# Cross attention of a fp32 transformer trunk: plain fp32 operands in scores and values in place of split halves of queries, keys, values and probabilities

## The reference

```python
def memory_cross_attention(h, mem_n, w_q, w_kv, w_o):
    B, S, _ = h.shape
    M = mem_n.shape[1]
    q = (h @ w_q).reshape(B, S, XA_HEADS, HEAD_DIM)
    kv = (mem_n @ w_kv).reshape(B, M, 2, XA_HEADS, HEAD_DIM)
    s = jnp.einsum('bshd,bmhd->bhsm', q, kv[:, :, 0]).astype(jnp.float32) * HEAD_DIM ** -0.5
    p = jax.nn.softmax(s, axis=-1)
    o = jnp.einsum('bhsm,bmhd->bshd', p.astype(kv.dtype), kv[:, :, 1])
    return o.reshape(B, S, XA_HEADS * HEAD_DIM) @ w_o
```

## Time and profile before

| what | value |
|---|---|
| median of 3 runs | 2618.49 us (2615.28 to 2619.13) |
| the profiled execution, its own time | 2622.67 us |
| its span, first to last instruction | 2620.9 us |
| mean granted TensorE clock in it, as a share of full speed | 0.966 |
| busy: TensorE, VectorE, ScalarE | 94%, 57%, 43% of the span |

### The profile page before, as it was taken

One profiled execution on the slowest core, in us unless ns is written; L12 is line 12 of the kernel. 1 busy time (PEld: TensorE's weight loads), 2 busy tenths in 40 slices (PEclk: granted clock), 3 DMA queues, 4 the chain that ended last, 5 costly groups with the idle time before them and its releaser, 6 DMA issues.

```text
span 2620.9 us, 38028 instructions
## 1 busy us (share of the span) xinstructions
PE 2473.1 (94%) x13452; PEld 2049.6 (78%) x13452; DVE 1505.3 (57%) x3239; ACT 1134.9 (43%) x2267; POOL 104.1 (4%) x178
## 2 busy tenths in 40 slices
PE   7999898999999899999999999989999988999998
PEld 5887687788778688888778877868878777888886
DVE  4668776672775555552265786757547555455423
ACT  5356563652644532222243564646346445222222
POOL 3000000000001100000000000000000101000000
PEclk8999998999999899999989999989999988999999
DMA  4221122123124013333322211221221420233332
GB/s 117 89 89 33 49 65 57 57 59 96 48 79 131 25 57 96 96 97 93 81 81 73 74 33 57 65 57 56 75 79 42 129 73 25 75 97 98 94 97 69
DMA packets 343960, 193.98 MB, mean 74 GB/s; under 512 B 29825, under 2 KB 339206, under 8 KB 343174
## 3 DMA queue, kind: packets, MB, share of 16 engines
q1 hardware_dynamic: 340512, 178.02, 23.7%
q0 software_dynamic: 2224, 13.67, 1.5%
q10 hardware_dynamic: 1078, 0.36, 0.1%
HBM read 184.69 MB, written 7.34 MB: 73 GB/s over the span
## 4 chain that ended last, share of the span: by engine, by line
PE 83%; DVE 8%; issue 4%; ACT 4%; POOL 1%; DMA 1%; DVEq 0%; POOLq 0%; ACTq 0%; SPq 0%
PE acc L1220 65%; PE o_acc L1220 5%; PE turn L1389 3%; PE scores L1220 3%; PE scores L1276 2%; ACT w_hi L772 2%; DVE ring L1960 1%; DVE w_lo L1702 1%; PE scores L1374 1%; DVE p_lo L1801 1%; PE o_acc L1298 1%; PE scores L1291 1%; PE scores L1375 1%; PE scores L1434 1%; DVE ring L1768 1%
## 5 line engine op out<-in xcount | busy, mean ns | idle before, releaser
L1702 DVE TENSOR_TENSOR w_lo<-w_f,w_hi 128x1024 fp32r<-128x1024 f32 x336 | 411.5, 1225 | 562.0 <-ACT w_hi L772 561.6
L1220 PE MATMUL acc<-h_hi,w_hi 128*128 128x512 f32 x1712 | 683.9, 399 | 11.1 <-DVE h_lo L1742 4.8
L1220 PE MATMUL acc<-h_hi,w_lo 128*128 128x512 f32 x1712 | 676.4, 395 | 0.0
L1220 PE MATMUL acc<-h_lo,w_hi 128*128 128x512 f32 x1712 | 676.3, 395 | 0.0
L772 ACT ACTIVATE w_hi<-w_f 128x1024 fp32r<-128x1024 f32 x336 | 353.7, 1053 | 267.7 <-PE acc L1220 262.2
L1220 PEld LDWEIGHTS acc<-h_hi,w_hi 128*128 128x128 f32 x1712 | 326.3, 191 | 73.4 <-issue 8.5
L1220 PEld LDWEIGHTS acc<-h_hi,w_lo 128*128 128x128 f32 x1712 | 325.6, 190 | 68.3
L1220 PEld LDWEIGHTS acc<-h_lo,w_hi 128*128 128x128 f32 x1712 | 326.4, 191 | 60.1
L825 ACT ACTIVATE p_hi<-turn 128x128 fp32r<-128x128 f32 (+3 forms) x356 | 149.3, 419 | 272.5 <-PE turn L1389 271.6
L1801 DVE TENSOR_TENSOR p_lo<-turn,p_hi 128x128 fp32r<-128x128 f32 (+3 forms) x356 | 165.8, 466 | 73.8 <-ACT p_hi L825 72.4
L913 ACT ACTIVATE ring<-ring,neg_max 128x128 f32<-128x128 f32 (+2 forms) x352 | 188.8, 536 | 37.7 <-DVE neg_max L1960 36.9
(11 more groups left out here) (311 smaller groups left out, 3758.1 us busy)
## 6 DMA issues: line engine op xcount, KB each, us to landing
w_f<-in_ffn_w_in_dram SPq DMA_DIRECT2D x88, 512.0 KB, 3.8
w_f<-in_w_gate_dram SPq DMA_DIRECT2D x64, 512.0 KB, 4.0
w_f<-in_w_in_dram SPq DMA_DIRECT2D x62, 512.0 KB, 3.8
w_f<-in_w_branch_dram SPq DMA_DIRECT2D x32, 512.0 KB, 3.4
w_f<-in_ffn_w_out_dram SPq DMA_DIRECT2D x32, 512.0 KB, 4.0
w_f<-in_w_out_dram SPq DMA_DIRECT2D x16, 512.0 KB, 4.1
w_f<-in_ffn_w_out_dram SPq DMA_DIRECT2D x16, 384.0 KB, 3.4
x_spill<-trunk POOLq DMA_DIRECT2D x2, 2048.0 KB, 7.7
```

The lines of the kernel that those rows point to most:

```text
L1220: ins = nc.tensor.matmul(dst, a, b, start=(n == 0 and not added), stop=(n == count - 1))
L1702: nc.vector.tensor_tensor(w_lo[:, u % 2, :], w_f32[:, u % 2, :], w_hi[:, u % 2, :].bitcast(F32), ALU.subtract).then_inc(w_ready, 1)
```

## The change

In the cross attention alone, scores are taken straight from the chunks of `proj_x` as one plain fp32 product of 64 by 128 by 256, and values as plain fp32 products of `p_whole` and `v_whole`, which lie where `p_hi` and `v_hi` lay. ScalarE's copies of the turned probabilities and values stay, now without the narrower format, and release TensorE themselves (`turn_ready`). Everything that made halves in this phase goes: `stage` on both engines, and `turn_rest` and `value_turns` on VectorE. `y_hi` and `y_lo` are made as before. Two waits of TensorE ahead of the phase are new; they are for copies of keys and values that were done some chunks earlier. Counters of semaphores are renumbered.

```diff
-ITEMS = [("nsa", 4), ("swa", 4), ("mla", 8), ("fox", 8), ("xa", XH)]
+WHOLE = ("v_xa", "xa")
+HIB, NHI = offsets([(name, 0 if name in WHOLE else n) for name, n in TURNS])
+
+ITEMS = [("nsa", 4), ("swa", 4), ("mla", 8), ("fox", 8)]
...
+        with ExitStack() as plain:
+            p_whole = sb("p_whole", [P, 2, S], F32, plain)
+            sb("p_gap", [P, 2, S], F32, plain)
+            v_whole = sb("v_whole", [P, NT, BW], F32, plain)
...
                 act.wait_ge(turned, t + 3)
-                nc.scalar.activation(dst, src, ACT.Copy).then_inc(turn_high, 1)
+                if name in WHOLE:
+                    if name == "v_xa" and k == 0:
+                        act.wait_ge(turn_ready, t + CREDIT)
+                    nc.scalar.activation(dst, src, ACT.Copy).then_inc(turn_ready, 1)
+                else:
+                    nc.scalar.activation(dst, src, ACT.Copy).then_inc(turn_high, 1)
...
-                    elif i == 0:
+                    elif i == 0 and ps is not XA:
                         pe.wait_ge(qk_ready, l * NIT + (IB[ps.name] + ps.item(h) + 1))
                     pe.wait_ge(biased, st + (s + 1))
                     bank, q = scores[s % 2][:, 0:w], slice(i * P, (i + 1) * P)
+                    if ps is XA:
+                        own = ps.half(h)
+                        nc.tensor.matmul(bank, proj_x[own, h // 2, q], proj_x[own, PJ_K["xa"] + h // 2, k0:k0 + w],
+                                         start=True, stop=True).then_inc(scored, 1)
+                        return
...
                     for t in range(n):
+                        if ps.name in WHOLE:
+                            ins = nc.tensor.matmul(o_acc[h % 2][0:HD, i * P:(i + 1) * P],
+                                                   v_whole[0:w, t0 + t, v0:v0 + HD],
+                                                   p_whole[0:w, s % 2, t * P:(t + 1) * P],
+                                                   start=(t == 0), stop=(t == n - 1))
+                            if t == n - 1:
+                                ins.then_inc(applied, 1)
+                            continue
...
                 wait_chunk_read(pe, l, "xq", 1)
+                wait_chunk_read(pe, l, "xkv", 2)
+                wait_chunk_read(pe, l, "xkv", 3)
                 attend(l, XA, (chunk_values("v_xa", PJ_V["xa"], MT, proj_x), 2))
...
             def value_turns(l, name, count, rows, tiles):
-                for n in range(count):
+                for n in range(0 if name in WHOLE else count):
...
-                    if 2 <= s <= ps.steps + 1:
+                    if 2 <= s <= ps.steps + 1 and ps.name not in WHOLE:
                         t = s - 2
```

More of the change, by code:

```diff
@@ L829, in value_turns @@
                     bank = turn[(TB[name] + n) % 2]
-                    turn_high_part(l, name, 0, n, v_hi[0:rows, 0:tiles, n * P:(n + 1) * P],
+                    turn_high_part(l, name, 0, n,
+                                   (v_whole if name in WHOLE else v_hi)[0:rows, 0:tiles, n * P:(n + 1) * P],
                                    bank[0:rows, 0:tiles * P].rearrange("p (t f) -> p t f", t=tiles))
@@ L921, in high @@
                         act.wait_ge(cmp_applied, 2 * KVH * (l + 1))
-                    turn_high_part(l, ps.name, 0, s, p_hi[0:rows, s % 2, 0:n * P],
+                    turn_high_part(l, ps.name, 0, s, (p_whole if ps.name in WHOLE else p_hi)[0:rows, s % 2, 0:n * P],
                                    turn[(TB[ps.name] + s) % 2][0:rows, 0:n * P])
@@ L1798, in turn_rest @@
             def turn_rest(l, name, n, k, dst, bank, high):
-                t = l * NTN + n + (TB[name] + k)
-                dve.wait_ge(turn_high, t + 1)
+                dve.wait_ge(turn_high, l * NHI + n + (HIB[name] + k + 1))
                 nc.vector.tensor_tensor(dst, bank, high.bitcast(F32), ALU.subtract).then_inc(turn_ready, 1)
             def value_turns(l, name, count, rows, tiles):
-                for n in range(count):
+                for n in range(0 if name in WHOLE else count):
                     bank = turn[(TB[name] + n) % 2][0:rows, 0:tiles * P].rearrange("p (t f) -> p t f", t=tiles)
@@ L1876, in block_values @@
                 bank = turn[TB["v_cmp"] % 2]
-                dve.wait_ge(turn_high, l * NTN + TB["v_cmp"] + 1)
+                dve.wait_ge(turn_high, l * NHI + HIB["v_cmp"] + 1)
                 for g in range(GROUP):
```

## The result

The changed kernel is slower: 2641.7 us, median of 4 runs (2636.53 to 2645.84), against 2618.39 us (2615.28 to 2619.13) for the kernel before on the same chips. The ratio is 1.009, 95% interval 1.0065 to 1.0115. The profiled execution took 2645.84 us with a span of 2643.7, 22.8 more than before.

What follows compares the result with a forecast made beforehand. In cross attention TensorE was taken to bind at half clock, VectorE with its handoffs at full. Full-clock savings of 12.7 us less 3.3 for slow stretches gave -9.4, from 2618.49 to 2609.1 us, range 2603.5 to 2615.5.

Steps and rivals of the forecast that it cites:

- the slow stretches: At the start of the cross attention phases: half-clock time halves from 17.0 to 8.5 us together, costing 3.3 us.
- Rival F: Cross attention: two-pass products don't bring the clock back, each layer 6 us slower, about 2631; chance 0.06.
- The step: TensorE's step in cross attention: from about 1.16 to 1.21 us at full clock, from 1.82 to 2.13 at half.
- rival E: Cross attention steps: weight loads don't hide, +13.8 us on -12.7, nothing gained (+1, between -2 and +4); chance 0.06.
- from the last `bias_scores` to the last `y_hi`: End of each phase: `turn_rest` leaves, `apply` lasts slightly longer; 0.4 us saved each, from 4.58 and 4.81.
- the outputs of the heads: Head outputs on ScalarE and VectorE use up TensorE's spare time: 0.4 us a head, 1.0 inside the 15 steps.
- The price of the records: Plain fp32 products on TensorE: four clock periods a column; score and `apply` 0.45 us each at full clock, 0.85 at half.
- The start: Phase start: first `bias_scores` 2.0 us earlier in the first layer, 1.7 in the second; under 1.5 behind the value transposes.
- the relief of VectorE: VectorE's own work in cross attention is 0.90 us a step, so TensorE at 1.21 sets the pace.
- The sum at full clock: Both cross attention phases at full clock throughout: -6.7 us in the first, -6.0 in the second, together -12.7.
- rival B: Cross attention at full clock throughout: -12.7 us, up to 1.5 more if a later slow stretch goes; chance 0.22.
- The 15 steps of a phase: First to last `bias_scores` at full clock: 15 x 1.21 + 1.0 = 19.2 us, -4.3 and -3.9.

Runs made afterwards that it cites:

- e1: Ten dummy products fill TensorE's idle time ahead of each cross attention phase in the changed kernel: 2637.39 us against 2617.26, ratio 1.0072.
- e3: Dummy products behind the changed kernel's end, time meaningless; plain blocks 1 (128 rows), 2 (64 weight columns), 3 (64 rows); step's mix 4 (score 64 rows), 5 (128).
- e8: Dummy blocks behind the changed kernel's end, time meaningless: one-pass 64 rows (1), plain upper 64 rows (3), plain 96 rows, 128 then 64 rows, alternating weight widths.
- e4: Only the values part of the change: values plain, scores in halves (128 rows, zero-padded) as before; 2612.96 us against 2618.36, ratio 0.9984.
- e5: Only the scores part of the change: scores plain on 64 rows, values in halves as before; 2640.26 us against 2618.36, ratio 1.009.
- e6: Changed kernel with scores of 128 rows, each head's keys padded with zeros; 2605.45 us against 2616.71, ratio 0.9953.
- e9: Changed kernel with values on 128 weight columns, scores still of 64 rows; 2641.47 us against 2618.25, ratio 1.0079.
- e7: On top of e6, values with 128 weight columns instead of 64, so no tile is partial; 2601.61 us against 2616.71, ratio 0.9942.

## Why the prediction was wrong

- *"I expect the slow stretches to halve": the step that failed.* They grew from 17 to 82 us, because a step with a score of 64 rows does not bring the clock back from 0.50 (and in e1's profiled execution let it fall from 1.00). Shown by e3 (block 3 against 1, block 4 against 5), e8 (blocks 1 and 3) and in the kernel by e4, e5, e6 and e9. My argument was that TensorE would be full from the second step on; it was, at 99%, and that did not matter. Rows 8, on which I leaned, are of transposes with 128 rows; in the whole trace of before no product of 64 rows runs at half clock.
- *Rival F* had the place, the sign and the point of decision (30 us at half clock; it was 82), but its cause falls: two-pass products of 128 rows do bring the clock back (e3, blocks 1 and 2), one-pass ones of 64 rows don't (e8, block 1). Its 2631 was 11 us short, since it took the step at 2.13 us. The Trainium skill, TensorE: Matmul & The Clock Gate, Part 1, has activity release the throttle; e3 agrees for 128 rows and shows that a busy array of 64 rows was not such activity.
- *The step: "the load of the transposed block hides behind a longer product".* Taken were 1.21 us at full clock and 2.13 at half; measured is 2.81 at half. Of the 0.68, 0.40 is the wait at the three changes of kind beyond the columns (0.136, 0.136 and 0.132), and 0.27 are loads that lie bare behind such waits: the first record of a kind takes 0.162 (score), 0.053 and 0.056 us longer to the next than its columns. Block 4 of e3 gives the same 2.81 with no other engine in play. This is rival E's thought, with another mechanism: loads do hide within a kind, and not at changes to or from a plain product that fills only part of the array. (The 0.92 us behind rival E's price stand in rows 7 for 7 records, and I divided by 8; the records start 0.112 apart, so its 0.115 is near all the same.) At full clock e6, with two such changes, has mostly 1.43, and e7 with none has 1.22 to 1.31 where TensorE sets the pace: the forecast's 1.21 nearly holds for full tiles.
- *By size:* of the 1.60 us by which a step exceeds the 1.21, 0.92 (2.13 - 1.21) are the clock and 0.68 the loads. The 12 steps of 2.81 in a phase make 12 x 1.60 = 19.2 us; with the 24.7 (31.4 - 6.7) forecast for a phase at full clock that is 43.9, measured 43.95 and 44.3. There is luck in so close a fit: from the last `bias_scores` to the last `y_hi` the first phase took 5.0 us, 0.8 more than forecast, and the 1.0 us set down for the outputs of the heads did not come.
- *The price of the records* was right: the first two `bias_scores` stand 0.43 us apart, against 0.45 forecast for a score at full clock, and a record of 256 columns takes 0.427 at half. Four periods a column agree with the Trainium skill, FP8 and Floating Point Precision, section TensorE Precision Notes, which gives true FP32 four passes.
- *The start* was right: 1.43 us from the transposes, under the 1.5 set. So was the relief of VectorE, and at half clock TensorE alone set the pace: `bias_scores` waited for `scores` 15 times, 21.9 us in all. At full clock that was right in part. In e7 TensorE was busy 86%, and its transposes waited 5 times for `ring`, 2.9 us in a phase.
- *The sum at full clock*, -12.7 us (rival B), is what e7 reaches once the tiles are full: phases of 24.5 us against the forecast 24.7, and 2601.61 - 2616.71 = -15.1 us. The 15 steps of a phase make 19.0 us, forecast 19.2; the split is another, with short steps first and longer ones later.

What stays open: why a load waits at such a change, why few rows keep the clock down, why two widths by turns do, and whether one cause stands behind both, why dense products of 64 rows kept a full clock that the mix of a step lost, and what a step of the change as written costs at a lasting full clock, since no profiled execution held it there (e1 shows 1.14 and 1.41 for the first steps only). That a partial tile, and not the kind of product, makes the load wait is read from pairs, and one pair does not fit it: from a one-pass product of full size to a plain one of full size the load also waits, the other way it does not.

## What to carry to other kernels

Before a product is put on part of the array (64 of 128 rows), look whether the stretch starts at half clock or can fall to it: here zeros in the other 64 rows, which cost TensorE no column, were worth 35 us against the same scores on 64 rows (11.3 faster than before instead of 23.3 slower; one waiting change less is in that). Read the granted clock of the stretch beside the busy share, since TensorE was 99% busy in the slowest phase and 86% in the fastest. Where kinds of products alternate, read the loads and not the products: a load that starts a product's length plus 0.13 us behind it, instead of at once, is a cost that the busy time hides.

## What the hardware showed unexpectedly

- Dense products of 64 rows kept 0.50 for 15.1 us in plain fp32 and 13.4 us in one pass (e3, e8); 96 rows had 1.00 after 6 us, 128 rows after 3.5. From full clock, 64 rows kept 1.00 for 9.6 us. Filling the other 64 rows with zeros was enough (e6).
- A stream of 128-row products of 64 and 128 weight columns by turns, in which the first load of each product waited, stayed at 0.50 for 32 us (e8).
- At every change met here between a plain product on part of the array and another kind (transposes, one-pass products, plain ones of another width), the next load starts only after the product's columns are through: 0.349 us after the start of a record of 0.213 at half clock (0.136 more), 0.201 after one of 0.109 at full (0.092 more).
- The number of rows has no part in the length of a product (0.427 us a record of 256 columns with 64 and with 128 at half clock, e3). The Trainium skill, TensorE: Matmul & The Clock Gate, section Why this matters for your kernels, says so of 32 rows; here the empty rows cost nothing in length and all in the clock.
